# Three float16 products for the tiles' output projection, two weight groups prepared in each pooling tile, and the sample keys side by side

## The chip, the cores and the metric

The kernel runs on one core of a Trainium2 chip. The metric is the device time of one execution in microseconds (us). The engines are TensorE (PE: matmuls, with their weight loads in a row of their own, PEld), VectorE (DVE), ScalarE (ACT), GpSimd (POOL), and SyncE (SP), whose queue issues most of the transfers. The engines run apart and wait for one another by semaphores; each executes its own instructions in the order in which they are written.

## What is computed

One inference step of a decoder of two layers, for a prompt of 2048 tokens and for a sample group of 8 x 8 tokens, with shared weights (width 1024). Each layer has one combined input projection, a token mixer, a cross-attention over 256 memory tokens, gates, and one output projection that is added to the residual:

```python
z = rms_norm(x, norm_a[i]) @ w_in_a[i]                      # 1024 -> 2048
u, gp, qm, gm = jnp.split(z, [POOL_W, 2 * POOL_W, 2 * POOL_W + MEM_W], axis=-1)
yp = pool_mixer(u_ext, pos, pool_mix_w[i], pool_scale[i]) * jax.nn.silu(gp)
ym = memory_branch(qm, gm, mem_q_norm[i], mem_k[i], mem_v[i])
x = x + jnp.concatenate([yp, ym], axis=-1) @ w_out_a[i]     # 1024 -> 1024
...
q = rope_partial(rms_norm(q.reshape(B, T, N_Q_HEADS, HEAD_DIM), q_norm[j]), pos)
o = swa_banded(q, k, v, sinks[j])            # sample group: swa_window over 128 cached + 8 new keys
ys = o * jax.nn.silu(gq)
x = x + jnp.concatenate([ys, ym], axis=-1) @ w_out_b[j]
```

Layer A mixes by pooling windows of 2, 4, 8 and 16 tokens; layer B by a sliding window of 128 tokens with sinks. All inputs and outputs are float32.

## The kernel before

The program has five parts, one after the other: a prologue ("pre": memory keys and values, the splitting of layer A's input weights), loop A (8 pooling tiles of 256 prompt tokens), the sample block of layer A (SA), loop B (8 window tiles) and the sample block of layer B (SB). Values lie feature-major, 128 partitions x 8 chunks x 256 tokens.

**The input projections** are already taken as three float16 products: a float32 weight group (1024 x 256, 1 MB) and the normalised inputs are each split into a high and a low float16 part, and high x high, high x low and low x high are summed in PSUM (`split_features`, L623; the query part `qm` of a pooling tile is L794). The parts of layer B's weights are made during loop A, one group of 1 MB in each pooling tile: SP loads it into `stage_b` (L486), GpSimd multiplies it by the norm's gain (`gained`, L2055), ScalarE takes magnitudes (L1200), a TensorE matmul spreads the largest of all to every partition (`largest`, L633), VectorE makes a scale of it, ScalarE and VectorE write the high and the low part (L1137, L1511), and SP stores them to HBM (L489).

**The output projection** (`by_feature`, L649; its first half group L823 in a pooling tile and L1027 in a window tile) is in float32: 4 output groups `out0` to `out3` of 2 halves x 8 chunks, 64 matmuls 128x128x256 in a tile. `add_outputs` (DVE, L1596) adds each group to the residual.

**Order.** Nothing schedules at run time: each engine's stream is written by hand, and rings of PSUM banks are handed on by semaphores (Z for projections, T for transposes and totals, S for scores, V for values). A pooling tile on TensorE is `qm`, `u0` to `u2`, query transposes, `g0` with the memory scores in it, `g1`, `g2` and `gm` with transposes in them, memory values, `out0` to `out3`. During the output groups the next tile's input is squared (ACT, L1110), summed (GpSimd, `sums`, L2031 to L2035), its square sums go through TensorE (`square_sums`, "ss", L589), GpSimd takes the power (L2026), and a second matmul (`rstd_rows`, "rb", L600) spreads the result; VectorE and ScalarE then write the next tile's normalised high and low parts (L1472/L1476, L1132, L1482).

## Time and profile before

| | |
|---|---|
| time, median of 3 runs | 1806.86 us (1805.43 to 1807.42) |
| the profiled execution | 1804.33 us, span 1802.5 us, mean granted TensorE clock 0.968 of full |
| TensorE busy | 1687.7 us (94% of the span) |
| VectorE, ScalarE, GpSimd busy | 700.3, 504.8, 458.4 us (39, 28, 25%) |
| prologue, up to the first pooling tile | 119.7 us |
| loop A, each tile | 77.1 us |
| sample block A | 79.6 us |
| loop B, each tile | 109.1 us |
| sample block B | 111.2 us |

The span is the part of the time in which the profile shows the engines at work; the rest lies around it. A tile's period is read from the start of its first projection to the start of the next tile's. Busy shares are averages over stages with different limits, so each stage is read by itself.

### The profile page before, as it was taken

The numbers are of one execution on the slowest core, as the hardware profiler recorded it, in microseconds if no ns is written. First come the engines' busy times: TensorE is split into PE (matmuls) and PEld (weight loads), VectorE is DVE, ScalarE is ACT, GpSimd is POOL, SyncE is SP. The second block draws the span as 40 slices with busy tenths as digits, with TensorE's granted clock in tenths as the row PEclk, the third lists the DMA queues.
The fourth block names the chain that finished last, engine by engine and source line by source line (L and its number), as shares of the span: only waits on it lengthen the run. The fifth ranks groups of instructions, "written<-read, shape, count | busy, mean of one in ns | idle before, by whom it ended". The sixth has DMA issues, their size and how long they took to land.

```text
span 1802.5 us, 29285 instructions
## 1 busy us (share of the span) xinstructions
PE 1687.7 (94%) x11586; PEld 1286.4 (71%) x11586; DVE 700.3 (39%) x1621; ACT 504.8 (28%) x1236; POOL 458.4 (25%) x344
## 2 busy tenths in 40 slices
PE   5769999999999999869999999999999999999967
PEld 3648888888888888734767757677675776757753
DVE  3643241422424233213624436353452634536320
ACT  3343132231322223112504224142331514215110
POOL 0214134141422414212313123031321313223010
PEclk9789999999999999989999999999999999999976
DMA  9132201102020120565010010100001010010211
GB/s 367 55 120 86 94 25 72 57 38 95 13 83 25 71 94 1 186 266 229 1 47 1 2 48 2 47 1 27 23 1 47 1 48 1 1 47 1 101 50 47
DMA packets 23477, 113.60 MB, mean 63 GB/s; under 512 B 2551, under 2 KB 2999, under 8 KB 12550
## 3 DMA queue, kind: packets, MB, share of 16 engines
q1 hardware_dynamic: 22046, 102.87, 14.8%
q10 hardware_dynamic: 1296, 8.76, 1.2%
q8 instruction: 106, 1.74, 0.4%
q14 instruction: 29, 0.24, 0.0%
HBM read 80.24 MB, written 33.44 MB: 63 GB/s over the span
## 4 chain that ended last, share of the span: by engine, by line
PE 45%; issue 36%; POOL 13%; DVE 2%; DMA 2%; ACT 1%; POOLq 0%; SPq 0%; ACTq 0%; DVEq 0%
PE ps_z L623 17%; PE ps_z L649 12%; POOL tiny_sb L2026 4%; POOL ph_sb L2147 3%; PE ps_z L794 2%; PE ps_z L640 2%; POOL pm_sb L2050 2%; POOL pm_sb L2061 2%; PE ps_z L823 2%; POOL big_sb L2031 1%; PE ps_z L612 1%; PE ps_t L589 1%; PE ps_s L661 1%; PE ps_p L679 1%; PE ps_t L669 1%
## 5 line engine op out<-in xcount | busy, mean ns | idle before, releaser
L623 PE MATMUL ps_z<-xn_sb,w_in_sb 128*128 128x256 f16 (+1 forms) x4752 | 499.8, 264 | 0.8 <-DVE pm_sb L1527 0.8
L623 PEld LDWEIGHTS ps_z<-xn_sb,w_in_sb 128*128 128x128 f16 x4752 | 426.6, 98 | 62.1 <-issue 14.7
L649 PE MATMUL ps_z<-gate_sb,w_out_sb 128*128 128x256 f32 x1792 | 396.0, 380 | 0.0
L649 PEld LDWEIGHTS ps_z<-gate_sb,w_out_sb 128*128 128x128 f32 x1792 | 337.4, 190 | 44.2
L2026 POOL TENSOR_TENSOR tiny_sb<-tiny_sb 128x2 f32<-128x2 f32 (+4 forms) x56 | 94.1, 1681 | 777.7 <-DVE tiny_sb L1533 595.0
L612 PE MATMUL ps_z<-w_in_sb,xn_sb 128*128 128x512 f16 (+2 forms) x840 | 181.7, 376 | 0.0
L1118 ACT ACTIVATE scr_sb<-ps_z,tiny_sb 128x256 f32<-128x256 f32 (+2 forms) x94 | 42.5, 489 | 408.8 <-PE ps_z L612 314.2
L612 PEld LDWEIGHTS ps_z<-w_in_sb,xn_sb 128*128 128x128 f16 (+1 forms) x840 | 82.9, 99 | 94.2 <-issue 0.3
L1596 DVE TENSOR_TENSOR x_buf_sb<-x_buf_sb,ps_z 128x512 f32<-128x512 f32 x64 | 44.0, 687 | 250.4 <-PE ps_z L649 250.4
L1524 DVE TENSOR_REDUCE tiny_sb<-scr_sb 128x8 f32<-128x512 f32 (+3 forms) x64 | 38.0, 594 | 239.2 <-ACT scr_sb L1118 166.1
L1551 DVE TENSOR_REDUCE tiny_sb<-ps_s 128x4 f32<-128x1024 f32 x32 | 39.0, 1219 | 171.2 <-PE ps_s L661 171.2
L1132 ACT ACTIVATE xn_sb<-big_sb 128x2048 f16<-128x2048 f32 x18 | 34.4, 1910 | 226.7 <-DVE big_sb L1476 148.7
L1353 ACT ACTIVATE ph_sb<-ph_sb,tiny_sb 128x128 f32<-128x128 f32 x192 | 74.6, 390 | 68.0 <-DVE tiny_sb L1868 68.0
L612 PE MATMUL ps_z<-w_x_sb,xn_sb 128*128 128x512 f16 (+1 forms) x408 | 89.8, 379 | 0.1
L2147 POOL TENSOR_TENSOR ph_sb<-ph_sb,tiny_sb 128x512 f32<-128x512 f32 x48 | 49.9, 1041 | 152.9 <-DVE tiny_sb L1878 152.9
L2061 POOL TENSOR_TENSOR pm_sb<-pm_sb,tiny_sb 128x1024 f32<-128x1024 f32 x32 | 60.2, 1893 | 93.9 <-DVE tiny_sb L1559 93.9
L1566 DVE SCALAR_TENSOR_TENSOR gate_sb<-scr_sb,ps_z 128x512 f32<-128x512 f32 (+1 forms) x72 | 45.9, 638 | 85.8 <-ACT scr_sb L1149 85.3
L1160 ACT ACTIVATE pm_sb<-ps_s,tiny_sb 128x256 f32<-128x256 f32 x128 | 58.5, 474 | 56.8 <-DVE tiny_sb L1554 56.8
L612 PEld LDWEIGHTS ps_z<-w_x_sb,xn_sb 128*128 128x128 f16 (+1 forms) x408 | 39.9, 98 | 47.8 <-issue 1.3
L2031 POOL TENSOR_TENSOR big_sb<-big_sb 128x1024 f32<-128x1024 f32 x17 | 39.9, 2350 | 121.6 <-ACT big_sb L1110 121.6
L1149 ACT ACTIVATE scr_sb<-ps_z,tiny_sb 128x512 f32<-128x512 f32 (+1 forms) x72 | 46.9, 651 | 80.0 <-PE ps_z L623 78.7
L1154 ACT ACTIVATE big_sb<-ps_t 128x512 f32<-128x512 f32 (+1 forms) x68 | 39.6, 582 | 95.1 <-PE ps_t L669 69.9
(262 smaller groups left out, 2091.3 us busy)
## 6 DMA issues: line engine op xcount, KB each, us to landing
x_buf_sb<-x SPq DMA_DIRECT2D x18, 1024.0 KB, 4.9
x<-x_buf_sb SPq DMA_DIRECT2D x9, 1024.0 KB, 3.9
y<-x_buf_sb SPq DMA_DIRECT2D x9, 1024.0 KB, 4.0
w_x_sb<-w_in_b SPq DMA_DIRECT2D x8, 1024.0 KB, 6.7
w_in_sb<-parts ACTq DMA_DIRECT2D x8, 1024.0 KB, 11.0
w_out_sb<-w_mem SPq DMA_DIRECT2D x4, 1024.0 KB, 18.7
w_out_sb<-w_out_a SPq DMA_DIRECT2D x4, 1024.0 KB, 8.2
parts<-ph_sb SPq DMA_DIRECT2D x8, 512.0 KB, 3.1
```

The lines of the kernel that those rows point to most:

```text
L612: last = mm(out, xs[:, x, kc, tok:tok + n], w[:, gs[0]:gs[-1] + 1, ws, kc, :], start=(kc == 0 and ws + x == 0), stop=(kc == KC - 1 and ws ...
L623: last = mm(ps_z[:, b, half * NT:half * NT + n], w_split[:, g, ws, kc, half * P:(half + 1) * P], xs[:, x, kc, 0:n], start=(kc == 0 and ws ...
L649: last = mm(ps_z[:, b, half * NT:half * NT + n], w[:, g, kc, half * P:(half + 1) * P], src[:, kc, 0:n], start=(kc == 0), stop=(kc == KC - 1))
L1149: f(pair[0], pair[1], ACT.Tanh, scale=halfunit).then_inc(scr_in.sem, 1)
L1160: last = f(pm[:, blk, e, :], ps_s[:, b, e // 2, (e % 2) * NMEM:(e % 2 + 1) * NMEM], ACT.Exp, bias=m_neg[:, blk, e:e + 1], scale=SCALE, acc ...
L1353: f(sw[:, n % 2, e, :], sw[:, n % 2, e, :], ACT.Exp, bias=w_neg[:, n % 2, e:e + 1], scale=SCALE, accum_out=w_sum[:, n % 2, e:e + 1])
L1566: ve.scalar_tensor_tensor(gate[:, c:c + 2, 0:n], pair[0], 1.0, pair[1], ALU.add, ALU.mult)\
L1596: ve.tensor_tensor(x, x, ps_z[:, b].rearrange("p (c n) -> p c n", c=2)[:, :, 0:n], ALU.add)\
L2026: return tt(out, x, power[0:n, 0:w], ALU.pow)
L2031: own(tt(big[:, 0:4], big[:, 0:4], big[:, 4:8], ALU.add))
L2061: tt(pm[:, blk], pm[:, blk], r, ALU.mult).then_inc(pm_norm.sem, 1)
L2147: tt(sw[:, i], sw[:, i], r, ALU.mult).then_inc(pw_norm.sem, 1)
```

## The change

1. The tiles' output projection is taken as three float16 products (`split_outputs`): the output weights are split once (layer A's 4 groups at the end of the prologue, layer B's in loop A, stored with the others), and each tile's gated values are split by ScalarE (`gate_high`) and VectorE (`gate_low`) in four pairs of chunks. 64 float32 matmuls of a tile become 192 float16 ones.
2. Loop A prepares two weight groups in each tile (16 slots: 8 input groups, the shared K/V and 4 output groups of layer B) and does so at the tile's start: both groups are loaded behind the next tile's x, GpSimd multiplies by the gain, VectorE takes the largest of each row (`row_top_of`), ScalarE squares and accumulates (`row_squares`), and a TensorE matmul between `u1` and `u2` adds over partitions (`totals`).
3. Square sums in loop A come after the whole of `out0`; the spread ("rb") after `out1`. In loop B they come after `out0` and `out1`, and the spread after `out2`.
4. In the prologue the same row tops take the place of ScalarE's magnitudes, and GpSimd's gain passes are gone.
5. The sample blocks keep the float32 output projection and load its weights for it: in SA 4 MB and the pooling mix (0.75 MB) come ahead of the state projection's second weight group.
6. In SB old and new keys lie side by side (136 columns for each batch), so that scores take one matmul pair where there were two, and the new values one matmul for each key pair instead of one for each batch; the memory attention comes ahead of the window's values.

The sync engine's queue:

```diff
+            def prepare(t):
+
+                for s in range(2):
+                    sp.wait_ge(parts_out.sem, parts_out.after("A", t, -1))
+                    dma(stages[s], one_slot(io["w_b"], t * 2 + s).rearrange("a p k n -> (a p) k n"))\
+                        .then_inc(stage_in[s].sem, 16)
+                for s in range(2):
+                    out = one_slot(io["parts"], t * 2 + s).rearrange("a p s k n -> (a p) s k n")
+                    for half in range(2):
+                        sp.wait_ge(low_in.sem, low_in.after("A", t, 2 * s + half))
+                        dma(out[:, :, half * 4:half * 4 + 4, :], parts_b[s][half])\
+                            .then_inc((parts_out if s + half else first_out).sem, 16)
 
...
+            sp.wait_ge(parts_out.sem, parts_out.total)
+            sp.wait_ge(first_out.sem, first_out.total)
+            dma(w_x[:, 0:1536], io["mix"]).then_inc(mix_reload, 16)
+            dma(stages[1], io["w_u"][0]).then_inc(wu_in, 16)
...
+            Z.wait_full(sp, "A", TILES - 1, "out3")
+            for g in range(4):
+                dma(w_out[:, g], io["w_out_a"][g]).then_inc(wout_in[g], 16)
```

TensorE, the new functions, a pooling tile and the end of a window tile:

```diff
+            def totals(part, t, k, name, parts):
+
+                pe.wait_ge(top_sum.sem, top_sum.after(part, t, k))
                 T.wait_free(pe, part, t, name)
...
+                mm(ps_t[:, 0:parts.shape[1]], ones[:, :], parts, start=True, stop=True).then_inc(T.full[0], 1)
...
+            def split_outputs(part, t, name, g, chunks=range(KC), halves=(0, 1), first=True, last=True):
+
+                b = Z.wait_free(pe, part, t, name) if first else Z.bank(part, name)
+                for half in halves:
+                    for kc in chunks:
+                        for ws, x in PARTS:
+                            start = first and half == 0 and kc == chunks[0] and ws + x == 0
+                            done = mm(ps_z[:, b, half * NT:(half + 1) * NT],
+                                      w_out_split[:, g, ws, kc, half * P:(half + 1) * P], gated_parts[:, x, kc, :],
+                                      start=start, stop=last and half == 1 and kc == chunks[-1] and ws == 1,
+                                      skip_group_check=True)
+                if last:
+                    done.then_inc(Z.full[b], 1)
+
+            def wait_gated(part, t, k):
+                pe.wait_ge(gated_low.sem, gated_low.after(part, t, k))
```

```diff
-                    for i in range(3):
-                        split_features("A", t, f"u{i}", 1 + i)
+                    split_features("A", t, "u0", 1)
+                    split_features("A", t, "u1", 2)
+                    totals("A", t, 1, "top", w_top)
+                    split_features("A", t, "u2", 3)
...
-                    for g in range(4):
-                        pe.wait_ge(wout_in[g], 32)
-                    pe.wait_ge(pool_gated.sem, pool_gated.after("A", t))
-                    b = Z.wait_free(pe, "A", t, "out0")
-                    for kc in range(KC):
-                        if kc == POOLC:
-                            V.wait_read(pe, "A", t, "pvm")
-                        mm(ps_z[:, b, 0:NT], w_out[:, 0, kc, 0:P], gate[:, kc, :], start=(kc == 0), stop=(kc == KC - 1))
-                    largest("A", t, 0, "top0")
-                    by_feature("A", t, "out0", gate, w_out, 0, halves=(1,))
+                    pe.wait_ge(low_in.sem, low_in.after("pre", 0, 11))
+                    wait_gated("A", t, 0)
+                    split_outputs("A", t, "out0", 0, (0, 1), last=False)
+                    wait_gated("A", t, 1)
+                    split_outputs("A", t, "out0", 0, (2, 3), first=False, last=False)
+                    wait_gated("A", t, 2)
+                    split_outputs("A", t, "out0", 0, (4, 5), first=False, last=False)
+                    wait_gated("A", t, 3)
+                    split_outputs("A", t, "out0", 0, (6, 7), first=False)
```

```diff
                     window_transposes(t, 4)
-                    V.wait_read(pe, "B", t, "pvw2")
-                    first_output((0, 1, 6))
+                    wait_gated("B", t, 1)
+                    split_outputs("B", t, "out0", 0, (0, 1, 6, 7), last=False)
                     window_values(t, p, 4)
                     window_transposes(t, 5)
-                    V.wait_read(pe, "B", t, "pvw3")
-                    first_output((7, 2, 3))
+                    wait_gated("B", t, 2)
+                    split_outputs("B", t, "out0", 0, (2, 3), first=False, last=False)
+                    split_outputs("B", t, "out1", 1, (0, 1), last=False)
                     window_values(t, p, 5)
-                    V.wait_read(pe, "B", t, "pvw5")
-                    first_output((4, 5))
-                    by_feature("B", t, "out0", gate, w_out, 0, halves=(1,))
+                    split_outputs("B", t, "out1", 1, (6, 7, 2, 3), first=False, last=False)
+                    wait_gated("B", t, 3)
+                    split_outputs("B", t, "out0", 0, (4, 5), first=False)
+                    split_outputs("B", t, "out1", 1, (4, 5), first=False)
                     square_sums(V, "B", t, "ss", 0)
-                    project_out("B", t, (1,))
+                    project_out("B", t, (2,))
                     rstd_rows("B", t, "rb", 0)
```

ScalarE:

```diff
+            def gate_high(part, t, k, pair):
+                if part == "A" and pair < 3:
+                    act.wait_ge(gated.sem, gated.after(part, t, pair))
+                else:
+                    V.wait_read(act, part, t, ("pvw1", "pvw3", "pvw5", "pvm")[pair])
+                f(gated_parts[:, 0, PAIRS[pair], :], gate[:, PAIRS[pair], :], ACT.Copy).then_inc(gated_high.sem, 1)
```

```diff
+                    pooled_inputs(0)
+                    row_squares(row_tops[:, 0, :], w_top[:, 0:1], "A", t, 0, 0)
+                    row_squares(row_tops[:, 1, :], w_top[:, 1:2], "A", t, 1, 1)
+                    pooled_inputs(1)
+                    high_b(t, 0, 0)
+                    high_b(t, 0, 1)
+                    pooled_inputs(2)
                     from_t("A", t, "qT", qT_a[:, :, :], ps_t[:, :].rearrange("p (c n) -> p c n", c=2))
+                    high_b(t, 1, 0)
...
+                    gate_high("A", t, 0, 0)
+                    gate_high("A", t, 1, 1)
+                    gate_high("A", t, 2, 2)
                     tanh("A", t, "gm", halfunit_a[:, 7:8])
-                    magnitudes(t)
+                    gate_high("A", t, 3, 3)
```

VectorE:

```diff
+            def gate_low(part, t, k, pair):
+                dve.wait_ge(gated_high.sem, gated_high.after(part, t, k))
+                ve.tensor_tensor(gated_parts[:, 1, PAIRS[pair], :], gate[:, PAIRS[pair], :], gated_parts[:, 0, PAIRS[pair], :],
+                                 ALU.subtract).then_inc(gated_low.sem, 1)
...
+                    for s in range(2):
+                        dve.wait_ge(w_gained.sem, w_gained.after("A", t, s))
+                        row_top_of("A", t, s, row_tops[:, s, :], stages[s])
+                    power_from("A", t, 0, "top", w_power)
+                    scale_from("A", t, 0, w_power, w_scale, [(unit_b[:, bass.ds(t * 2, 2)], w_power, 1.0 / X_UNIT)])
+                    low_b(t, 0, 0)
+                    low_b(t, 0, 1)
                     for blk in range(NBLK):
                         mem_max("A", t, blk)
+                    low_b(t, 1, 0)
                     for blk in range(NBLK):
                         mem_inverse("A", t, blk)
-
-                    dve.wait_ge(parts_out.sem, parts_out.after("pre", 0, 1))
+                    low_b(t, 1, 1)
...
-                    window_differences(t)
-                    mix_gated("A", t)
+                    gate_low("A", t, 0, 0)
+                    mix_gated(t, 2)
+                    gate_low("A", t, 1, 1)
+                    gate_low("A", t, 2, 2)
                     silu("A", t, "gm", 4, 6)
                     mem_gated("A", t)
-                    weight_top("A", t, 0)
-                    weight_scale("A", t, 0, "top0", unit_b[:, bass.ds(t, 1)])
```

GpSimd:

```diff
+            def gained(t, s):
+
+                pool.wait_ge(stage_in[s].sem, stage_in[s].after("A", t))
+                gains = sm("slotgain")[:, bass.ds((t * 2 + s) * KC, KC)]
+                tt(stages[s], stages[s], gains.rearrange("p (k n) -> p k n", n=1).to_broadcast([P, KC, 256]), ALU.mult)\
                     .then_inc(w_gained.sem, 1)
+
...
+                    gained(t, 0)
                     heads("A", t, 0, q_rstds[0][:, 0:8], q_of(0)[:, 0:8, :], unit_a[:, 0:1].to_broadcast([P, 8]))
+                    gained(t, 1)
+                    weight_power("A", t, 0, w_power)
```

TensorE in SB, the window's values:

```diff
+                mm(ps_p[:, 0:384].rearrange("p (b n) -> p b n", b=DB), v[0:NS, 0, kp * P:(kp + 1) * P], pt_new[:, :, cols],
+                   start=True, stop=False, skip_group_check=True)
                 for n in range(DB):
-                    out = ps_p[:, n * 48:(n + 1) * 48]
-                    mm(out, v_old[:, n, kp * P:(kp + 1) * P], pt_old[:, n, cols], start=True, stop=False)
-                    last = mm(out, v_new[:, n, kp * P:(kp + 1) * P], pt_new[:, n, cols], start=False, stop=True)
+                    last = mm(ps_p[:, n * 48:(n + 1) * 48], v_old[:, n, kp * P:(kp + 1) * P], pt_old[:, n, cols],
+                              start=False, stop=(n == DB - 1), skip_group_check=True)
                 last.then_inc(V.full[0], 1)
```

How the order moves. TensorE from `qm` to the query transposes in a pooling tile, before (`ps_z` holds projections, `ps_t` transposes and totals):

```order
L794 MATMUL ps_z<-w_in_sb,xn_sb 128x256 x47
L623 MATMUL ps_z<-xn_sb,w_in_sb 128x256 [waits z_free1]
L623 MATMUL ps_z<-xn_sb,w_in_sb 128x256 x47
L124 REGISTER_ALU
L623 MATMUL ps_z<-xn_sb,w_in_sb 128x256 [waits z_free0]
L623 MATMUL ps_z<-xn_sb,w_in_sb 128x256 x47
L623 MATMUL ps_z<-xn_sb,w_in_sb 128x256 [waits z_free1]
L623 MATMUL ps_z<-xn_sb,w_in_sb 128x256 x47
L776 REGISTER_ALU
L124 ISA [waits heads_norm]
L780 MATMUL ps_t<-small_sb,pm_sb 128x128 [waits t_free]
L780 MATMUL ps_t<-small_sb,pm_sb 128x128 x3
```

and now:

```order
L654 MATMUL ps_z<-xn_sb,w_in_sb 128x256 x47
L128 REGISTER_ALU
L654 MATMUL ps_z<-xn_sb,w_in_sb 128x256 [waits z_free0]
L654 MATMUL ps_z<-xn_sb,w_in_sb 128x256 x47
L662 ISA
L128 ISA [waits top_sum]
L664 MATMUL ps_t<-tiny_sb,ones_sb 128x2 [waits t_free]
L654 MATMUL ps_z<-xn_sb,w_in_sb 128x256 [waits z_free1]
L654 MATMUL ps_z<-xn_sb,w_in_sb 128x256 x47
L832 REGISTER_ALU
L128 REGISTER_ALU [waits heads_norm]
L836 MATMUL ps_t<-small_sb,pm_sb 128x128 [waits t_free]
```

Between the second and the third pooled projection stands a matmul of 128x2 that waits for the row sums of both weight groups (`top_sum`).

GpSimd from a pooling tile's first instruction, before (`pm_sb` holds queries and memory weights, `ph_sb` the pooling windows):

```order
L2026 TENSOR_TENSOR tiny_sb<-tiny_sb 128x8 [waits heads_var]
L163 ISA
L2047 TENSOR_TENSOR tiny_sb<-tiny_sb 128x8 [waits pool_steps]
L163 REGISTER_ALU
L2050 TENSOR_TENSOR pm_sb<-pm_sb,tiny_sb 128x512 [waits pool_steps]
L134 ISA
L2105 TENSOR_TENSOR ph_sb<-ph_sb 128x6x270 [waits z_free0,z_free1]
L163 REGISTER_ALU
L2107 TENSOR_TENSOR ph_sb<-ph_sb 128x5x268 [waits pool_steps]
L2059 ISA
L2061 TENSOR_TENSOR pm_sb<-pm_sb,tiny_sb 128x1024 [waits m_inv_in]
```

and now:

```order
L2234 ISA [waits stage_in0]
L2234 TENSOR_TENSOR w_x_sb<-w_x_sb,small_sb 128x2048
L2220 REGISTER_ALU
L2203 TENSOR_TENSOR tiny_sb<-tiny_sb 128x8 [waits heads_var]
L167 ISA
L2224 TENSOR_TENSOR tiny_sb<-tiny_sb 128x8 [waits pool_steps]
L167 REGISTER_ALU
L2227 TENSOR_TENSOR pm_sb<-pm_sb,tiny_sb 128x512 [waits pool_steps]
L2234 ISA [waits stage_in1]
L2234 TENSOR_TENSOR w_x_sb<-w_x_sb,small_sb 128x2048
L138 ISA
L2203 TENSOR_TENSOR tiny_sb<-tiny_sb 128x2 [waits t_free]
```

Two gain passes over 128x2048 and a power stand ahead of the windows, the first of them ahead of the query heads; the pass that stood behind the windows is gone.

TensorE at the last windows of a window tile, before (`ps_p` holds window values):

```order
L942 MATMUL ps_t<-small_sb,ph_sb 128x128 [waits t_free,pw_norm]
L942 MATMUL ps_t<-small_sb,ph_sb 128x128 x3
L1027 MATMUL ps_z<-gate_sb,w_out_sb 128x256 [waits p_free]
L1027 MATMUL ps_z<-gate_sb,w_out_sb 128x256 x2
L134 REGISTER_ALU
L124 REGISTER_ALU [waits t_free]
L954 MATMUL ps_p<-ph_sb 64x128 [waits p_free]
L954 MATMUL ps_p<-ph_sb 64x128 x7
L939 REGISTER_ALU
L942 MATMUL ps_t<-small_sb,ph_sb 128x128 [waits t_free,pw_norm]
L942 MATMUL ps_t<-small_sb,ph_sb 128x128 x3
L1027 MATMUL ps_z<-gate_sb,w_out_sb 128x256 [waits p_free]
```

and now:

```order
L685 REGISTER_ALU
L128 REGISTER_ALU [waits gated_low]
L677 MATMUL ps_z<-pm_sb,w_out_sb 128x256 [waits z_free0]
L677 MATMUL ps_z<-pm_sb,w_out_sb 128x256 x23
L138 REGISTER_ALU
L128 REGISTER_ALU [waits t_free]
L1013 MATMUL ps_p<-ph_sb 64x128 [waits p_free]
L1013 MATMUL ps_p<-ph_sb 64x128 x7
L998 REGISTER_ALU
L1001 MATMUL ps_t<-small_sb,ph_sb 128x128 [waits t_free,pw_norm]
L1001 MATMUL ps_t<-small_sb,ph_sb 128x128 x3
L685 REGISTER_ALU
```

The first output matmuls now wait for the low parts of the gated values (`gated_low`), 24 of them in a row stand ahead of the fifth window's values.

## Rows read from the trace of the kernel before

**Rows 1.** Windows: start:end, length, busy by engine, clock, DMA share, GB/s.

```profile
0.00:119.92 119.92, 77.56 (x251) 51.31 (x252) 64.55 (x116) 48.80 (x45) 14.35 (x14) 0.86 0.39 160
430.16:507.29 77.13, 77.13 (x576) 67.48 (x575) 26.03 (x55) 19.68 (x35) 24.45 (x16) 1.00 0.14 56
739.12:818.73 79.61, 58.94 (x560) 35.71 (x559) 14.28 (x40) 13.04 (x29) 14.77 (x26) 0.87 0.69 262
1036.76:1145.90 109.14, 106.15 (x711) 75.86 (x711) 49.11 (x121) 33.67 (x103) 28.02 (x21) 1.00 0.06 20
1691.30:1802.50 111.20, 84.73 (x523) 53.73 (x522) 20.67 (x58) 14.45 (x53) 9.73 (x8) 0.74 0.22 80
```

**Rows 2.** TensorE's timeline in pooling tile 4: start, busy, operation, count.

```profile
430.00 5.40 PE L794 MATMUL ps_z<-w_in_sb,xn_sb 128*128 128x256 f16 x48
435.24 15.88 PE L623 MATMUL ps_z<-xn_sb,w_in_sb 128*128 128x256 f16 x144
...
493.31 13.98 PE L649 MATMUL ps_z<-gate_sb,w_out_sb 128*128 128x256 f32 x64
```

**Rows 3.** Sync engine's queue, same tile, and the page's issues (median us to landing).

```profile
435.60 0.33 SPq L486 DMA_DIRECT2D w_x_sb<-w_in_b  x1
...
w_x_sb<-w_in_b SPq DMA_DIRECT2D x8, 1024.0 KB, 6.7
```

**Rows 4.** GpSimd's timeline, same tile.

```profile
437.60 1.64 POOL L2026 TENSOR_TENSOR tiny_sb<-tiny_sb 128x8 f32<-128x8 f32 x1 [27.65 <-DVE tiny_sb L1533]
439.59 1.04 POOL L2050 TENSOR_TENSOR pm_sb<-pm_sb,tiny_sb 128x512 f32<-128x512 f32 x1
...
467.35 3.60 POOL L2055 TENSOR_TENSOR w_x_sb<-w_x_sb,small_sb 128x2048 f32<-128x2048 f32 x1
480.79 2.35 POOL L2031 TENSOR_TENSOR big_sb<-big_sb 128x1024 f32<-128x1024 f32 x1 [9.84 <-ACT big_sb L1110]
...
484.56 0.73 POOL L2035 TENSOR_TENSOR big_sb<-big_sb 128x256 f32<-128x256 f32 x1
```

**Rows 5.** VectorE's and ScalarE's timelines, same tile.

```profile
487.51 1.28 DVE L1511 SCALAR_TENSOR_TENSOR ph_sb<-w_x_sb,tiny_sb,ph_sb 128x1024 f16<-128x1024 f32 x1
...
501.02 2.28 DVE L1482 TENSOR_TENSOR xn_sb<-big_sb,xn_sb 128x2048 f16<-128x2048 f32 x1
...
478.81 1.90 ACT L1110 ACTIVATE big_sb<-x_buf_sb 128x2048 f32<-128x2048 f32 x1
```

**Rows 6.** GpSimd's and VectorE's timelines in a window tile.

```profile
1094.71 1.89 POOL L2061 TENSOR_TENSOR pm_sb<-pm_sb,tiny_sb 128x1024 f32<-128x1024 f32 x1 [4.17 <-DVE tiny_sb L1559]
...
1095.76 0.86 DVE L1876 TENSOR_TENSOR tiny_sb<-tiny_sb 128x4 f32<-128x4 f32 x1 [0.70 <-ACT tiny_sb L1355]
...
1103.65 0.16 DVE L1876 TENSOR_TENSOR tiny_sb<-tiny_sb 128x4 f32<-128x4 f32 x1 [1.42 <-ACT tiny_sb L1355]
```

**Rows 7.** Windows in the prologue, and TensorE's first pooling projection.

```profile
75.10:77.40 2.30, 0.00 (x0) 0.01 (x1) 2.20 (x4) 2.30 (x2) 0.00 (x0) 1.00 0.00 0
78.50:82.00 3.50, 3.24 (x9) 2.13 (x7) 3.50 (x4) 0.14 (x1) 0.00 (x0) 0.51 0.00 0
...
119.72 7.00 PE L794 MATMUL ps_z<-w_in_sb,xn_sb 128*128 128x256 f16 x48
```

**Rows 8.** TensorE's and VectorE's timelines where a window tile ends.

```profile
1112.87 1.46 PE L1027 MATMUL ps_z<-gate_sb,w_out_sb 128*128 128x256 f32 x6
...
1113.07 1.29 DVE L1886 TENSOR_TENSOR ph_sb<-ps_t,small_sb 128x512 f32<-128x512 f32 x2
```

**Rows 9.** TensorE's waits in the first sample block.

```profile
PE ps_z L724 <- DMA w_x_sb<-w_u: 7.4, 1, 7.4
```

**Rows 10.** Groups by line, TensorE, in the second sample block.

```profile
L1091 PE MATMUL ps_p<-w_in_sb,w_x_sb 128*128 128x48 f32 x32 | 10.6, 431 | 2.6 <-DVE gate_sb L2011 1.5 <-DVE w_in_sb L2000 1.1
L1092 PE MATMUL ps_p<-w_in_sb 8*128 8x48 f32 x32 | 10.5, 426 | 0.0
L1066 PE MATMUL ps_s<-ph_sb,w_in_sb 128*96 128x8 f32 x32 | 5.3, 308 | 1.9 <-ACT w_in_sb L1194 1.9
```

668 lines of the change are left out of this document (390 added, 278 removed).

## The prediction

> **What bounds the kernel now.** I read the page's busy shares first, then windows for each stage, since the share is an average over five different parts. [rows 1] give one pooling tile, one window tile and the three blocks outside the loops. In a pooling tile TensorE is busy 77.13 of 77.13 us; VectorE, ScalarE and GpSimd have 26.0, 19.7 and 24.5 us of work. There nothing but TensorE counts, and its time falls only if its instructions get shorter and nothing makes it wait. In a window tile it is busy 106.15 of 109.14. In the first sample block it is busy 58.9 of 79.6 with the DMA engines at 0.69, in the second 84.7 of 111.2 at a clock of 0.74: waits set those. So the view to ask next is the timeline of one tile, in order to see which chain could reach TensorE late.
>
> **The output projection.** [rows 2] have both kinds of matmul on 128x128x256. The float32 row has two records for each matmul, so its 64 records are 32 matmuls in 13.98 us, 0.437 us each. 144 float16 ones take 15.88 us, 0.110 each, at the same clock of 1.00. Old: 64 x 0.437 = 28.0 us in a tile. New: 192 x 0.110 = 21.1. That is **-6.9 us** in a pooling tile. In a window tile, where the first half group was cut into pieces of three and two matmuls at 0.487 ([rows 8]: 6 records in 1.46), 28.4 becomes 21.1: -7.3. Sixteen tiles would give 114 us if no wait came with it.
>
> **The wait for the two weight groups.** The totals matmul stands between `u1` and `u2`, and TensorE takes instructions in order: all of `u2` and the rest of the tile queue behind it. With E the start of `qm`, `u0` starts at E+5.24 and a group of 48 takes 5.23 [rows 2], so TensorE is there at E+15.7. The operand comes by this chain: the x load must wait for the x store of the tile that just ended, so the queue reaches the weight load at E+5.60 [rows 3], and its median landing time is 6.7 us. Two loads now share the queue; I put 0.7 on the first: landed at E+13.0. Then GpSimd in its written order: gain 3.60, query heads 3.03 (437.60 to 440.63), gain 3.60 [rows 4], E+23.2. Row tops of the second group on VectorE: no such row; the nearest of 2048 elements takes 2.28 [rows 5], E+25.5. Squares and accumulation of 128x8 on ScalarE, about 0.4, and two handoffs: E+26.3. TensorE stands **10.6 us**. Bounds: 8.8 (the first load alone, a cheaper reduction) and 12.8 (row tops held up behind GpSimd). None of it can move into the tile before, since the loads follow the store that follows the last `out3`.
>
> **After a wait the clock is low.** In [rows 7] TensorE did nothing for 2.30 us, and the stretch just after ran at 0.51, which is 1.2 GHz instead of 2.4. The first pooling projection, after 11.65 us without work, took 7.00 where the same 48 matmuls take 5.40 in tile 4: 1.6 us lost. I charge **+1.6** for the 10.6 us wait (bounds 0.5 to 3). The Trainium skill says the same of idle time in "TensorE: Matmul & The Clock Gate" (Part 1: The HAM clock gate); by it a cold array runs at 1.2 GHz; the trace agrees, with 0.51 after 2.30 us idle, and the 7.00 us row is already the price.
>
> **Further on in the pooling tile.** (a) The squares of the next x now stand on ScalarE behind `gate_high` of the last pair, which waits for the memory branch: they end at about 481.9 on the old axis, and the sums take 4.5 more (480.79 to 485.29, [rows 4]), to 486.4. TensorE, which comes to `out0` at 478.1 and now some 0.4 later (b), has finished all of it, 48 x 0.110, at 483.75: a wait of **+2.65** where there was none, and about +0.9 for the clock (half of the 1.7 that a full low stretch would cost). (b) `g2` waits for `silu g0`, which VectorE does behind the fourth low part: **+0.4**. (c) That low part reads two SBUF tiles. In [rows 6] a 128x4 VectorE instruction with two SBUF inputs takes 0.86 instead of 0.16: it ends at 1096.62, and the GpSimd instruction that it lay beside ends at 1096.60. The low part (1.28, [rows 5]) falls beside the memory normalisation on GpSimd, 1.89 each: **+1.2** (0 if it meets a gap). The Trainium skill has this as a lock, in "SBUF — State Buffer" (Who interferes with whom): a VectorE instruction with two SBUF inputs and a GpSimd one that reads SBUF exclude each other until the first ends; the trace agrees to 0.02 us, and without that rule the tile would be 1.2 shorter. (d) The low part of the next x is ready about 2 us before `out3` ends: no wait.
> Sum for a pooling tile: -6.9 + 10.6 + 1.6 + 2.65 + 0.9 + 0.4 + 1.2 = **+10.45**, 77.1 to 87.6. Seven tiles: **+73**.
>
> **Prologue and first tile.** Four more weight groups are split after the first 8 (ScalarE 1.90, VectorE 2.28 each, [rows 5]), and the queue's loop starts only when the last is done. I put that at 133 (119.7 and four times 2.3, behind some 4 us of totals and heads); then 7 us to the landing and the chain above, 14 us, so `u2` of tile 0 starts at about 154.8 where it now starts at 137.0 (119.72 and 6.83 for `qm` [rows 7], two groups of 5.23): **+17.8**, with 4 either way. The rest of that tile is -6.9 and the terms (a) to (c), -0.1 with a low-clock wait: -0.1.
>
> **First sample block.** 4 MB of output weights and 0.75 MB of mix stand in the queue ahead of the state projection's second group. TensorE already waits 7.4 us there for such a group [rows 9]; at some 400 GB/s the new bytes are 12 us, of which the wait at the value slots later on (the block has 20 us without TensorE work) absorbs part. I take **+4.5** (1 to 10).
>
> **Window tiles.** Besides -7.3, four small waits at the window outputs (1.1 together, of the 3.0 us idle in [rows 1]) go. New: the first 24 matmuls want the low part of pair 3, which VectorE does behind the weights of window 4: these end at 1114.36 ([rows 8], 1113.07 + 1.29), plus 0.7 for the subtraction, 1115.1, and TensorE is there at 1112.87: **+2.2**. Queued behind on TensorE are the values of windows 4 and 5; nobody else waits for them so early. The spread after `out2` leaves only `out3` (5.3 us) to cover VectorE 2.28, ScalarE 1.90 and VectorE 2.28 [rows 5] plus handoffs, 6.8: **+1.55**. Clock after the 2.2: 0.9 (0 to 1.7). Sum -3.75, eight tiles: **-30** (-24 to -39).
>
> **Second sample block.** 64 value matmuls [rows 10] of 0.43 become 16 + 2 wider pairs: from 21.1 us to about 12. The two score passes become one over 136 columns: some 5 us of the 5.3 [rows 10]. Gates fill waits at the transposes, some 4 us; the merged softmax and the memory waits give a few back: **-11** (-5 to -16).
>
> **Sum.** +73 + 17.8 - 0.1 + 4.5 - 30 - 11 = +54.2 on the profiled 1804.3: 1858.5. The median of the runs shown lies 2.5 above the profiled execution, so **1861 us**. Differences under 0.2% (3.6 us) can't be told from none.
>
> **Rivals.**
> *The chain is short (faster).* If the operand reached TensorE by E+20 (loads that land sooner, GpSimd passes that overlap), the wait would be 4 us and, at a wait that short, the clock loss about half: a tile gains 0.4 + what (a) leaves, so it is about +3; with B and SB at their better ends and the first tile at +12 that is 21 + 12 + 2 - 36 - 14 = -15: about 1792. It decides at a wait of about 3.5 us in a tile with the other terms as forecast, at 5.5 with all of them at those better ends. Against it: [rows 3] and [rows 4] alone, without any of VectorE's work, put the chain at E+23.2. **0.13.**
> *No clock loss.* The array keeps 2.4 GHz after the waits: 8 x 2.5 in A and 8 x 0.9 in B less, 27 us: about 1833. Against it stand both kinds of stretch in [rows 7]. **0.12.**
> *The waits cost more.* Row tops or the low parts meet GpSimd's passes more often, and the wait is at 12.8: seven tiles at +13, and B loses 3 more at its `gate_low` subtractions, which also read two SBUF tiles: about 1890. **0.15.**
> *The products gain nothing*: 192 float16 matmuls behind `gate_low` waits are as slow as 64 float32 ones; then 114 us more, near 1970. Against it the 0.110 of [rows 2], from the very same shape: **0.02.**
>
> **How the numbers follow.** The forecast has 0.58; by itself its bounds give 1840 to 1880. The range that leaves out no more than 2 in 10 takes in the case without clock loss and the costly one, and reaches toward the short chain: 1808 to 1892. Faster by over 0.2%: the first rival, 0.13. Same: 0.04, taken from the low end of the second. Slower: 0.83.
>
> **What would show it.** In the profile after: output matmuls at about 0.110; in each pooling tile a wait of 9 to 13 us on TensorE ahead of the totals matmul, put down to ScalarE's row sums or to what feeds them, with a clock near 0.5 after it; a wait of 2 to 3 at the square sums; tiles of 86 to 89; window tiles of 104 to 107. I am wrong if the totals wait is under 5 us, if a window tile's new waits exceed 7, or if the second sample block does not get shorter.

## The result, and the profile after

The changed kernel takes **1885.86 us** in the median of four runs (1878.95 to 1888.27) where the kernel before takes 1806.14: a ratio of 1.044, with an interval of 1.042 to 1.046. It is slower, as forecast; 1861 was named, within 1808 to 1892. The profiled execution took 1888.27 us.

The page of the kernel after opens like this:

```profile
span 1886.4 us, 31792 instructions
...
PE 1610.1 (85%) x12555; PEld 1203.0 (64%) x12555; DVE 814.6 (43%) x1733; ACT 544.3 (29%) x1344; POOL 500.5 (27%) x365
```

Its windows (columns as in [rows 1]) are, in order: prologue, pooling tiles 0, 1 and 4, the first sample block, one window tile, the second sample block.

```profile
0.00:121.73 121.73, 73.50 (x254) 48.47 (x255) 67.55 (x114) 42.99 (x52) 12.78 (x17) 0.88 0.45 179
121.73:213.86 92.13, 76.39 (x639) 64.80 (x640) 44.75 (x86) 26.46 (x45) 30.70 (x19) 0.89 0.15 60
213.86:304.08 90.22, 74.04 (x640) 63.43 (x638) 37.05 (x62) 22.67 (x43) 29.70 (x18) 0.92 0.18 71
484.42:574.23 89.81, 74.94 (x638) 63.99 (x639) 35.54 (x60) 22.56 (x43) 29.70 (x18) 0.90 0.18 71
841.27:929.18 87.91, 59.14 (x560) 36.10 (x559) 14.42 (x40) 13.06 (x29) 14.82 (x26) 0.84 0.76 293
1035.49:1142.09 106.60, 100.78 (x773) 71.00 (x773) 51.98 (x125) 36.16 (x108) 28.04 (x21) 0.98 0.06 21
1786.42:1886.40 99.98, 71.22 (x463) 40.62 (x463) 19.17 (x57) 15.56 (x57) 10.04 (x9) 0.79 0.36 131
```

A pooling tile was 77.1 us of TensorE without a gap at a clock of 1.00. It is now about 90, of which TensorE works 74 to 75, at 0.90 to 0.92. So the work shrank by less than the forecast 6.9 us, since some of it runs at the low clock, and 15 us of waiting came in. The window tile shown is 2.5 shorter, the second sample block 11.2, the first sample block 8.3 longer.

TensorE's timeline of pooling tile 1 shows where they stand (in brackets: the idle time ahead of the row and what ended it):

```profile
213.86 5.40 PE L850 MATMUL ps_z<-w_in_sb,xn_sb 128*128 128x256 f16 x48
219.10 10.64 PE L654 MATMUL ps_z<-xn_sb,w_in_sb 128*128 128x256 f16 x96
240.52 0.58 PE L664 MATMUL ps_t<-tiny_sb,ones_sb 128*128 128x2 f32 x2 [10.78 <-ACT tiny_sb L1273]
240.97 6.67 PE L654 MATMUL ps_z<-xn_sb,w_in_sb 128*128 128x256 f16 x48
...
262.04 2.79 PE L654 MATMUL ps_z<-xn_sb,w_in_sb 128*128 128x256 f16 x24 [1.02 <-DVE gate_sb L1667]
...
283.97 0.61 PE L620 MATMUL ps_t<-ones_sb,big_sb 128*128 128x1 f32 x4 [2.74 <-POOL big_sb L2212]
284.44 7.07 PE L677 MATMUL ps_z<-pm_sb,w_out_sb 128*128 128x256 f16 x48
...
304.08 0.61 PE L850 MATMUL ps_z<-w_in_sb,xn_sb 128*128 128x256 f16 x4 [1.65 <-issue]
```

The chain behind the 10.78 us, in the timelines of the sync engine's queue, GpSimd, VectorE and ScalarE for the same tile:

```profile
214.98 0.38 SPq L525 DMA_DIRECT2D x<-x_buf_sb  x1
219.04 0.35 SPq L522 DMA_DIRECT2D x_buf_sb<-x  x1
219.68 2.14 SPq L508 DMA_DIRECT2D w_x_sb<-w_b  x2
...
227.49 3.60 POOL L2234 TENSOR_TENSOR w_x_sb<-w_x_sb,small_sb 128x2048 f32<-128x2048 f32 x1 [28.68 <-DMA w_x_sb<-w_b]
...
234.06 3.60 POOL L2234 TENSOR_TENSOR w_x_sb<-w_x_sb,small_sb 128x2048 f32<-128x2048 f32 x1
...
237.69 2.29 DVE L1591 TENSOR_REDUCE tiny_sb<-w_x_sb 128x8 f32<-128x2048 f32 x1 [4.28 <-POOL w_x_sb L2234]
...
240.21 0.19 ACT L1273 ACTIVATION_READ_ACCUMULATOR tiny_sb<-tiny_sb 128x1 f32 x1
```

It is read backwards: totals at 240.52, row sums until 240.40, row tops until 239.98, the second gain pass until 237.66, the first from 227.49, when its load landed, and that load was issued at 219.68, since the x load ahead of it had to wait until the x store (214.98) was done. The two passes, the query heads between them and the row tops are in sequence; nothing in them is slow.

TensorE's waits over pooling tiles 1 to 7 and, behind the dots, over the window tiles (in total, times, longest):

```profile
PE ps_t L664 <- ACT tiny_sb L1273: 72.2, 7, 11.2
PE ps_t L620 <- POOL big_sb L2212: 19.2, 7, 2.7
PE ps_z L654 <- DVE gate_sb L1667: 7.1, 7, 1.0
PE ps_z L850 <- issue: 5.4, 3, 2.1
...
PE ps_z L677 <- DVE pm_sb L1616: 16.9, 8, 2.2
PE ps_z L643 <- DVE xn_sb L1588: 13.3, 8, 2.3
...
PE ps_z L643 <- issue: 5.8, 3, 2.0
```

The first three and the first two of the second part were forecast. The two rows "issue", 5.4 and 5.8 us, were not: TensorE waits for nothing that the profile shows, three times in each loop, just behind the loop's branch back, ahead of the first matmul in loop A and of the fifth in loop B (a loop body holds two tiles; the kernel before has 0.3 us of it at this line of loop A in all).

### The profile page after: what moved, and what is told of

It reads as the page before. It is cut to its first block, busy times and chain, and to the rows that moved or that the text cites. A ratio compares the mean times of both kernels' runs of the same rounds, so it can differ in the third digit from the quotient of the medians.

```text
span 1886.4 us, 31792 instructions
## 1 busy us (share of the span) xinstructions
PE 1610.1 (85%) x12555; PEld 1203.0 (64%) x12555; DVE 814.6 (43%) x1733; ACT 544.3 (29%) x1344; POOL 500.5 (27%) x365
## 4 chain that ended last, share of the span: by engine, by line
PE 41%; issue 21%; DVE 15%; POOL 11%; DMA 7%; ACT 4%; SPq 0%; POOLq 0%; DVEq 0%; ACTq 0%
PE ps_z L677 15%; PE ps_z L643 14%; DMA w_x_sb<-w_b 3%; PE ps_z L654 3%; DVE ph_sb L2055 2%; PE ps_z L691 2%; DVE ph_sb L2028 2%; ACT ph_sb L1443 2%; DVE tiny_sb L2031 2%; DMA x<-x_buf_sb 2%; POOL w_x_sb L2234 2%; POOL pm_sb L2245 1%; POOL tiny_sb L2203 1%; POOL ph_sb L2296 1%; POOL big_sb L2208 1%
## 5 line engine op out<-in xcount | busy, mean ns | idle before, releaser
L654 PE MATMUL ps_z<-xn_sb,w_in_sb 128*128 128x256 f16 (+1 forms) x4752 | 519.0, 270 | 8.6 <-DVE gate_sb L1667 8.1
L654 PEld LDWEIGHTS ps_z<-xn_sb,w_in_sb 128*128 128x128 f16 x4752 | 437.0, 101 | 79.3 <-issue 14.7
L677 PE MATMUL ps_z<-pm_sb,w_out_sb 128*128 128x256 f16 x3072 | 366.0, 282 | 16.9 <-DVE pm_sb L1616 16.9
L677 PEld LDWEIGHTS ps_z<-pm_sb,w_out_sb 128*128 128x128 f16 x3072 | 308.9, 102 | 66.8 <-issue 23.3
L2203 POOL TENSOR_TENSOR tiny_sb<-tiny_sb 128x8 f32<-128x8 f32 (+4 forms) x70 | 106.4, 1519 | 581.2 <-DVE tiny_sb L1634 267.8
L2234 POOL TENSOR_TENSOR w_x_sb<-w_x_sb,small_sb 128x2048 f32<-128x2048 f32 x16 | 57.6, 3603 | 231.3 <-DMA w_x_sb<-w_b 231.3
L1705 DVE SCALAR_TENSOR_TENSOR x_buf_sb<-ps_z,tiny_sb,x_buf_sb 128x512 f32<-128x512 f32 x64 | 47.9, 748 | 116.0 <-PE ps_z L677 116.0
L664 PE MATMUL ps_t<-tiny_sb,ones_sb 128*128 128x2 f32 (+3 forms) x28 | 6.9, 314 | 93.6 <-ACT tiny_sb L1273 84.8
L1591 DVE TENSOR_REDUCE tiny_sb<-w_x_sb 128x8 f32<-128x2048 f32 x17 | 38.8, 2285 | 108.0 <-POOL w_x_sb L2234 108.0
L664 PEld LDWEIGHTS ps_t<-tiny_sb,ones_sb 128*128 128x128 f32 x28 | 6.2, 267 | 98.3 <-issue 87.1
## 6 DMA issues: line engine op xcount, KB each, us to landing
w_in_sb<-parts ACTq DMA_DIRECT2D x8, 1024.0 KB, 11.1
```

The lines of the kernel that those rows point to most:

```text
L654: last = mm(ps_z[:, b, half * NT:half * NT + n], w_split[:, g, ws, kc, half * P:(half + 1) * P], xs[:, x, kc, 0:n], start=(kc == 0 and ws ...
L677: done = mm(ps_z[:, b, half * NT:(half + 1) * NT], w_out_split[:, g, ws, kc, half * P:(half + 1) * P], gated_parts[:, x, kc, :], start=sta ...
L1705: ve.scalar_tensor_tensor(x, ps_z[:, b].rearrange("p (c n) -> p c n", c=2)[:, :, 0:n], out_unit[part][:, g:g + 1], x, ALU.mult, ALU.add).t ...
L2203: return tt(out, x, power[0:n, 0:w], ALU.pow)
L2234: tt(stages[s], stages[s], gains.rearrange("p (k n) -> p k n", n=1).to_broadcast([P, KC, 256]), ALU.mult)\
```

## The experiments

Two theories were held against each other. **T1**: the loss comes from the waits of the forecast, each from the place where an edit put a step; move the step and the time comes back. **T2**: the float16 products bring the loss themselves (low clock, stalls at the branch, more matmuls behind each handoff), and it stays when the waits go. Ratios are to the kernel before on the same chip (1802.2 to 1803.6 us).

**1. Weight loads ahead of the store.** Both loads are issued behind the parts of the tile before, and the two gain passes run without the query heads between them; in the last tile two spare slots are loaded that nobody uses.

```diff
                     prepare(t)
+                    load_stages(t + 1)
...
                     gained(t, 0)
-                    heads("A", t, 0, q_rstds[0][:, 0:8], q_of(0)[:, 0:8, :], unit_a[:, 0:1].to_broadcast([P, 8]))
                     gained(t, 1)
+                    heads("A", t, 0, q_rstds[0][:, 0:8], q_of(0)[:, 0:8, :], unit_a[:, 0:1].to_broadcast([P, 8]))
```

> The changed kernel with the two weight loads of a pooling tile issued in the tile before (behind the stores of its weight parts, ahead of the x store), and GpSimd's two gain passes one behind the other ahead of the query heads. Theory (the wait at the totals is made by loads that follow the x store, and GpSimd's passes behind them): the 10.8 us wait ahead of the 128x2 totals matmul goes in tiles 1 to 7, and with it most of the low clock behind it (1.4 to 2.0); a pooling tile falls from 89.6 to about 77.3, tile 0 by about 3 (heads no longer stand in its chain), the whole to about 1797 us. Rival (the wait is VectorE's or ScalarE's place in the order, not the load): TensorE still waits over 5 us there and the kernel stays above 1840.

Measured: **1810.10 us**, ratio 1.003 (1.001 to 1.005), 76 us less than the changed kernel. Tiles 1 to 7 take 77.9 to 80.2 us. Its waits over the pooling tiles and the first sample block no longer have the totals matmul, and have one new row:

```profile
PE ps_t L629 <- POOL big_sb L2221: 19.2, 7, 2.7
PE ps_s L902 <- DMA x_buf_sb<-mem_ks: 12.1, 1, 12.1
PE ps_z L663 <- DVE gate_sb L1676: 9.0, 7, 1.3
PE ps_p L640 <- DVE diag_sb L1567: 7.3, 5, 3.0
```

The new wait is a collision that the early passes bring. VectorE's timeline in the changed kernel, then VectorE's and GpSimd's here, all in tile 1:

```profile
285.59 0.48 DVE L1558 TENSOR_SCALAR diag_sb<-small_sb,tiny_sb 128x128 f32<-128x128 f32 x2 [0.81 <-POOL tiny_sb L2203]
...
271.01 7.18 DVE L1567 TENSOR_SCALAR diag_sb<-small_sb,tiny_sb 128x128 f32<-128x128 f32 x2 [0.81 <-POOL tiny_sb L2212]
...
270.95 7.16 POOL L2243 TENSOR_TENSOR w_x_sb<-w_x_sb,small_sb 128x2048 f32<-128x2048 f32 x2
```

Two instructions that take 0.48 us together in the changed kernel take 7.18 here and end with the two gain passes beside them (278.19 and 278.11). The Trainium skill says in "SBUF — State Buffer" (Who interferes with whom) that a `tensor_scalar` can enter a mode with two ports, and that it and GpSimd then exclude each other for a whole instruction; this trace agrees, to 0.08 us. In experiment 6, where the passes wait until the diagonals are made, the row is gone. So T1 holds for the largest term. Of the 12 us by which tiles 1 to 7 miss the expectation, 7.3 are this wait and 1.9 a longer one ahead of `g2` (9.0 instead of 7.1); the rest was not taken apart.

**2. Squares ahead of the last high part.** ScalarE squares the next x before it makes `gate_high 3`.

```diff
-                    gate_high("A", t, 3, 3)
                     V.wait_full(act, "A", t, "pvm")
                     squares_x("A", t, 0, 1 - p, it * 16 + 32)
+                    gate_high("A", t, 3, 3)
```

> The changed kernel with ScalarE's squares of the next x ahead of the last gate_high in a pooling tile. Theory (the 2.74 us wait at the square sums comes from squares that stand behind gate_high of pair 3): the squares start about 1.8 us earlier, the wait falls to about 0.9 and the low clock behind it (1.67 in most tiles) goes in most tiles; 8 tiles by about 2.8 each, to about 1863 us. Rival (the last piece of out0 waits for its low part instead): the wait moves to the output matmuls and the time stays within 5 us of 1886.

Measured: 1868.43, 1.036 (1.034 to 1.038). TensorE's timeline in tile 1:

```profile
279.81 1.48 PE L677 MATMUL ps_z<-pm_sb,w_out_sb 128*128 128x256 f16 x12 [0.95 <-DVE pm_sb L1616]
281.73 0.61 PE L620 MATMUL ps_t<-ones_sb,big_sb 128*128 128x1 f32 x4 [0.43 <-POOL big_sb L2212]
282.20 5.40 PE L677 MATMUL ps_z<-pm_sb,w_out_sb 128*128 128x256 f16 x48
```

Of the 2.74 us wait 0.43 is left, 0.95 moved to the last quarter of `out0`, whose low part now comes later, and the next 48 matmuls are at 5.40 again instead of 7.07: 3.0 us in this tile. Tiles 1 to 7 got shorter by 2.2 us each, since the totals wait, which no line of this edit touches, was 0.7 a tile longer in this execution (77.3 us instead of 72.2). The clock's part, 1.67, is more than the forecast's 0.9.

**3. Padding at the branch.** Six float32 matmuls of 256 columns, into a result that nobody reads, at the end of each second pooling tile: 10 us more work in all, in order to see whether the "issue" time hides behind queued work.

```diff
+                    if p == 1:
+                        for _ in range(6):
+                            mm(ps_t[:, 0:NT], ones[:, :], gate[:, 0, :], start=True, stop=True)
```

> The changed kernel with six further float32 matmuls 128x128x256, whose result nobody reads, at the end of loop A's body on TensorE (every second tile, ahead of the branch back): 6 x 0.437 = 2.6 us of work in four places. Theory (the 1.65 to 2.13 us in which TensorE stands behind the branch, waiting for nothing shown, is time in which its sequencer gets to the new instructions, and short float16 matmuls leave too little queued work to cover it): the gap ahead of the query projection in tiles 2, 4 and 6 goes or falls under 0.5, and the total grows by only some 3 to 5 us. Rival (the gap is a fixed cost at that place or a wait for another engine): the gap stays at 1.6 to 2.1 and the total grows by 10.5.

Measured: 1871.83, 1.037 (1.035 to 1.040): more work, 14 us less time than 1885.86. The theory nearly holds: the "issue" time ahead of tiles 2, 4 and 6, 5.4 us before, is

```profile
PE ps_z L850 <- issue: 1.8, 3, 0.9
```

with 2.6 us of float32 matmuls ahead of the branch. The kernel before also has float32 matmuls there, and no stall. (The padding moves the code behind it too, but experiment 4 moves the code alone and keeps 6.0 us.) So this stall does come with the short products. Two more things happened that were not asked for. The totals wait in tiles 2, 4 and 6 is 6.4 to 6.7 us, where the changed kernel has 11.2, 11.1 and 6.3; but the same kernel run once more has 6.4, 6.6 and 11.2 without padding, so this is not shown to be the padding's work. And loop B, in which no line differs, lost its three stalls at the fifth matmul and went from 857.2 to 846.5 us. So these depend on something that changes when code ahead of them grows.

**4. Code shifted.** Six matmuls of one column, ahead of loop A, do nothing but move the instructions behind them. 30 of them move the same code further.

```diff
+            for _ in range(6):
+                mm(ps_p[0:64, 0:1], ones[:, 0:64], ones[:, 0:1], start=True, stop=True)
```

> The changed kernel with six tiny matmuls (12 instructions, 0.1 us each at most) on TensorE ahead of loop A, in the prologue, that write a PSUM bank nobody uses then: the loop bodies are the same, only moved in the program. Theory (the stalls behind the branches depend on where in the program's memory the instructions lie, which is how padding loop A alone took 11 us off loop B): the stalls of 1.7 to 2.0 behind the fourth matmul of the window tiles 2, 4 and 6 go, and the total falls by 8 to 12 us; in loop A they change place or size. Rival (loop B was faster in the padded run for another reason, its store or its waits): the stalls stay as in the changed kernel and the time stays within 3 us of it.

> The changed kernel with 30 tiny matmuls (60 instructions) ahead of loop A where the earlier run had 6. Theory (where a stall behind a branch falls hangs on the position of the instructions in program memory): the stalls of loop A or B sit at another matmul than the first and the fifth, or one of the two loops loses or gains one; the total differs from the run with 6 (1870) by several us. Rival (anything ahead of the loops takes the stalls of loop B away, or the difference was one of chip and run): the same picture as with 6.

> The changed kernel once more, as it is, beside the next two on one chip: 1880 to 1888 us by its earlier runs, with the same stalls behind the branches (1.65 to 2.13 in loop A, 1.7 to 2.0 in loop B).

Measured: **1869.95** (1.036, 1.034 to 1.038) with six, **1872.33** (1.038, 1.036 to 1.041) with 30, and the changed kernel once more 1883.78 (1.045, 1.042 to 1.047). The rows for "issue" in loop A, of the kernel with six and of the one with 30:

```profile
PE ps_z L853 <- issue: 6.0, 3, 2.2
```

```profile
PE ps_z L853 <- issue: 10.6, 6, 2.3
```

In loop B neither has any such row, and B takes 846.3 and 846.1 us, where the changed kernel took 857.2 and, run once more, 854.3: 8 to 11 us. What went is the stall at the fifth matmul. The one ahead of the first matmul stays in both loops; in B it lies inside the wait for the normalised inputs, which is 1.7 to 2.2 us behind a branch and 1.5 elsewhere. With 30, loop A has a second stall behind each branch, at the 25th matmul. So the second stall follows where the code lies, and the first does not.

The Trainium skill says in "Runtime: NRT & Kernel Launch" (Instruction fetch mechanics) that a taken branch to code that isn't at hand waits for a DMA fetch of it. The trace agrees as far as it goes: a packet of an instruction queue starts shortly before TensorE runs out of work. This is the queue's row (packets, MB, share) from 301.0 to 302.4 us in the changed kernel, whose TensorE works until 302.44 and then stands until 304.08:

```profile
q8 instruction: 1, 0.02, 4.2%
```

The kernel before has such a packet at the same branch (272.5 to 273.5 us) and no stall, for its TensorE works without a gap until the next tile begins at 275.73:

```profile
q8 instruction: 1, 0.02, 7.2%
```

The trace does not name the engine whose instructions come so. But the fetch stands at both branches, and with experiment 3 this says that the first stall comes where less work is left to cover it. No run here shows how much code is at hand, or what position makes a second stall. Loop A's tiles 1 to 7 take 622.1 us with six matmuls instead of 627.4, but kernels with an unchanged loop A took 624.2 (run once more) and 632.1 (the second kernel of experiment 5), so no gain there is shown.

**5. The end of a window tile.** The order of output pieces is changed so that pairs 0 and 3 come first and each waits only for its own low part, the square sums stand ahead of the last pair, and the spread stands in the middle of `out2`; VectorE takes the variance of x ahead of the first output sum.

```diff
-                    wait_gated("B", t, 1)
-                    split_outputs("B", t, "out0", 0, (0, 1, 6, 7), last=False)
+                    wait_gated("B", t, 0)
+                    split_outputs("B", t, "out0", 0, (0, 1), last=False)
+                    wait_gated("B", t, 1)
+                    split_outputs("B", t, "out0", 0, (6, 7), first=False, last=False)
...
+                    square_sums(V, "B", t, "ss", 0)
                     wait_gated("B", t, 3)
...
-                    project_out("B", t, (2,))
+                    split_outputs("B", t, "out2", 2, halves=(0,), last=False)
                     rstd_rows("B", t, "rb", 0)
+                    split_outputs("B", t, "out2", 2, halves=(1,), first=False)
```

> The changed kernel with three moves at the end of a window tile: the first 12 output matmuls wait only for the low part of pair 0 and the next 12 for that of pair 3; the square sums stand ahead of the last output pieces of out0 and out1; the spread of the result stands after the first half of out2. Theory (a window tile gains only 2.3 instead of 7.3 because of the 2.06 us wait for the low parts, the low clock after it, 1.7, and the 1.5 to 2.3 us wait for the next normalised inputs): the first wait falls to about 0.8, the clock stays up, the last wait goes; about 4.5 in a tile, 36 in eight, to about 1850 us. Rival (VectorE or ScalarE is late elsewhere in the same stretch, so the waits move): less than 10 us in all.

Measured: 1863.79, 1.0325 (1.031 to 1.034), where 1850 was expected. The first and the last window tile, which have no stall, take 101.6 us instead of about 106; the others take 103.3 to 103.6 or 106.1 to 108.9, as a part of a stall or most of it falls into them. The stalls behind a branch grew, from 5.8 to 17.0 us in the "issue" rows. The timelines of TensorE and the sync engine's queue:

```profile
1137.33 1.03 PE L643 MATMUL ps_z<-w_x_sb,xn_sb 128*128 128x512 f16 x4 [1.87 <-issue]
1142.85 12.34 PE L643 MATMUL ps_z<-w_x_sb,xn_sb 128*128 128x512 f16 x44 [4.48 <-issue]
...
1136.28 0.34 SPq L575 DMA_DIRECT2D y<-x_buf_sb  x1
```

The 1 MB y store goes out just as TensorE stalls. In a further kernel the store is held back until the next tile's first group is done:

```diff
+                    Z.wait_full(sp, "B", t + 1, "kv0")
                     dma(tile_of(yd, t), x_buf[:, 1 - p])
```

> The kernel with the new window end (1863.8 us) with the y store of a window tile held back until the next tile's first projection is complete, loop A untouched. Theory (instructions by DMA behind the store): the 6.3 us (1.9 and 4.5) that TensorE stands at the start of window tiles 2 and 6, and 4.5 at tile 4, fall to about 2; total 10 to 14 us less, about 1851. Rival (fixed cost, or a wait for another engine that the profile doesn't show): the stalls stay and the total stays within 3 us.

Measured: 1862.15, 1.031 (1.029 to 1.033). The "issue" rows of loop B, without and with the store held back:

```profile
PE ps_z L643 <- issue: 17.0, 6, 4.5
```

```profile
PE ps_z L644 <- issue: 11.0, 6, 2.3
```

So the store lengthens the stalls by 6 us over three branches; loop B gets 5.1 us shorter. The other 11 us are there without it: the 1.7 to 2.3 ahead of the first matmul, which the wait for the normalised inputs no longer hides, and the second stall. The whole got only 1.6 us shorter, not 10 to 14, and that lies within the spread of the runs.

**6. All together.** Edits 1, 2 and 5; GpSimd's gain passes wait until the diagonals are made; the output weights of loop A are loaded behind the first value slots of the sample block instead of ahead of them.

```diff
+                    pool.wait_ge(diag_x.sem, diag_x.after("A", t, -1))
                     gained(t, 0)
...
             for n in range(4):
                 load_slot(sp, "SA", n, 0, 1)
-            Z.wait_full(sp, "A", TILES - 1, "out3")
-            for g in range(4):
-                dma(w_out[:, g], io["w_out_a"][g]).then_inc(wout_in[g], 16)
...
             dma(stages[1], io["w_u"][2]).then_inc(wu_in, 16)
+            Z.wait_full(sp, "A", TILES - 1, "out3")
+            for g in range(4):
+                dma(w_out[:, g], io["w_out_a"][g]).then_inc(wout_in[g], 16)
             for n in range(12, 16):
```

> The early loads, the squares first and the new window end together, with two more edits: GpSimd's first gain pass waits until VectorE has written the diagonal tiles of the tile before (with the early loads alone TensorE stood 1.3 to 3.0 us for these, which I put down to the gain pass that VectorE's instruction lay beside), and the first sample block's output weights are loaded behind the third group of the state projection. If the waits were separate and of the sizes seen in the single runs: 1810 - 12 (diagonals) - 15 (squares) - 20 (window end) - 6 (sample block) = about 1757 us, below the kernel before. If they only pass one wait on to another: above 1790.

Measured: **1746.69**, 0.968 (0.966 to 0.970), 10 us under the sum of the single gains. Pooling tiles of 73.4 us, and 75.2 with a branch's stall at the end; the first sample block 80.2 instead of 87.9. Two variants followed: both stores held back, and the y store held back with the six matmuls of experiment 4.

> The combined kernel with the 1 MB store of a finished tile (x in loop A, y in loop B) held back until the next tile's first projection is complete. Theory (behind the branch of a loop TensorE waits for instructions that come by DMA, and these stand behind the store on the same DMA engines): the stalls ahead of and just behind the first projection of tiles 2, 4 and 6 (1.7 to 2.1 in loop A, 6.3 in loop B with the new window end) fall to 2 or less; about 10 to 15 us less than the combined kernel. Rival (the stalls are a fixed cost of the branch): no difference, or slower by what the later x loads cost.

> The combined kernel with the y store alone held back in loop B (the x store of loop A at its old place, since holding it back cost 7 us in the first sample block) and the six tiny matmuls ahead of loop A. Theory (position and store both stand behind the stalls): the window tiles behind a branch fall from 108.2 to about 104, loop A as in the combined kernel; about 12 us below its 1746.7, some 1735. Rival: the moved code puts the stalls elsewhere, 1742 to 1747.

Measured: 1744.43, 0.966 (0.9645 to 0.968), for the first, no clear gain over 1746.69: window tiles with a stall got 1.1 to 3.1 us shorter, but the last x store, held back, stands ahead of the sample block's loads in the queue: its first slot loads go out 8.7 us after the block's start instead of 5.6, and the block takes 87.6 instead of 80.2. The second took **1729.85**, 0.959 (0.957 to 0.961), the fastest kernel here. In its loop B the "issue" time falls from 18.0 us in six stalls to 6.6 in three: the first stalls are left. Its windows of pooling tile 2 and the first window tile:

```profile
280.55:353.95 73.40, 70.64 (x638) 61.73 (x639) 37.37 (x60) 22.66 (x43) 30.33 (x18) 1.00 0.23 86
811.16:912.74 101.58, 98.94 (x773) 70.17 (x773) 53.75 (x141) 35.85 (x107) 27.99 (x21) 1.00 0.22 84
```

The clock is back at 1.00, TensorE's work in pooling tile 2 is 70.6 us, 6.5 under the old 77.1, and 2.8 us of waits are left. T2 falls as the main cause: with the waits gone the products pay. What it has right is the first stall behind each branch.

## Why the prediction was right, point by point

**The wait for the two groups** was right in place, cause and size: E+26.66 for the totals in tile 1 where E+26.3 was worked out, and 72.2 us in seven tiles, 10.3 each, where 10.6 was forecast. Experiment 1 shows the cause: loads that don't follow the store, with the query heads' 3 us taken out from between the passes, remove it. The rival of a short chain is out.

**The clock** was right in kind, and so the rival without loss is out. After the long wait the 48 matmuls of `u2` took 6.67 to 7.73 us in tiles 1 to 7 where 5.40 is the price at full clock: 1.3 to 2.3 lost, 1.9 on average, forecast 1.6. After the wait at the square sums the loss is all or nothing: 1.67 in tiles 1 to 7 (7.07 instead of 5.40), and nothing in tile 0 behind a wait of the same length:

```profile
197.23 0.61 PE L620 MATMUL ps_t<-ones_sb,big_sb 128*128 128x1 f32 x4 [2.76 <-POOL big_sb L2212]
197.70 5.40 PE L677 MATMUL ps_z<-pm_sb,w_out_sb 128*128 128x256 f16 x48
```

The 0.9 that was charged, half of a figure that the rows before the change do not show, was too little here. In the window tiles, behind waits of 2.1 to 2.2, five tiles lost 1.67 and three nothing, 1.05 a tile where 0.9 was forecast; tiles 1 and 2:

```profile
1113.83 4.46 PE L677 MATMUL ps_z<-pm_sb,w_out_sb 128*128 128x256 f16 x24 [2.06 <-DVE pm_sb L1616]
...
1224.05 2.79 PE L677 MATMUL ps_z<-pm_sb,w_out_sb 128*128 128x256 f16 x24 [2.17 <-DVE pm_sb L1616]
```

What decides between the two, no run shows. Nor does the low stretch of [rows 7] stand just behind its wait, as the prediction reads it; 1.1 us of work at full clock lie between:

```profile
77.40:78.50 1.10, 1.07 (x5) 0.83 (x6) 1.10 (x1) 0.15 (x1) 0.00 (x0) 1.00 0.00 0
```

**The smaller terms of a pooling tile.** The wait at the square sums was 2.74, forecast 2.65. `g2` waited 1.02, where 0.4 and 1.2 were forecast: the low part did meet the memory normalisation, but took 2.09 instead of 1.28, 0.8 more. The sum was 87.6; tiles 1 to 7 take 627.4 us, 89.6 each. They lose 87 against the old 540.6, forecast 73. The missing 2 us a tile are the clock, the stalls (5.4 in seven tiles, 0.8 each) and the products, less 0.8 by which the three waits together were shorter than forecast. TensorE works 523.4 us in these tiles; the first kernel of experiment 6, at a clock of 1.00, works 495.1, and the kernel before 540.3. So the low clock took 4.0 a tile where 2.5 was forecast, and the products saved 6.5 instead of 6.9.

**Prologue and first tile** cost 15.4 us (213.86 against 198.44), forecast 17.7 (the working's own 133, 7 and 14 give 154.0 for `u2`, not 154.8). **The first sample block** cost 8.3, within its bounds of 1 to 10, but at another place than named: `w_u` still waits 6.9 [rows 9], and the wait for the key slots grew from 4.5 to 12.1, before and after:

```profile
PE ps_s L837 <- DMA x_buf_sb<-mem_ks: 4.5, 1, 4.5
...
PE ps_s L893 <- DMA x_buf_sb<-mem_ks: 12.1, 1, 12.1
```

The new bytes weren't absorbed by the slots; they are what the slots wait for: in experiment 6, with the weights behind them, this wait is 4.3 and the block takes 80.2 (84.1 in the fastest kernel, which waits 5.6 for the value slots). The prediction's 400 GB/s stands in no row; the 262 GB/s at a DMA share of 0.69 in [rows 1] make 380.

**Window tiles** are the term that was mis-sized: -15.4 us where -30, with bounds of -24 to -39, was forecast. The two waits were nearly right, 2.1 (2.2) and 1.7 (1.55), and so was the clock after the first. The stalls were not in the sum at all: 5.8 us of standing, and some 5 of low clock behind them (with the stall the first 48 matmuls of a tile take 14.0 to 14.3 us, in the others 10.5). Code shifted by six matmuls takes them away and gives 10.9 us back (8.1 against the changed kernel run once more), -26.3 in all, which is inside the bounds. The other 4 us are about 1 of clock after the first wait and about 3 of products that, by the fastest kernel's window tiles, saved 6.9 a tile instead of 7.3.

**The second sample block** gave 11.2, forecast 11, but its parts were rougher than that. The value matmuls saved 10.5 us (9 forecast; the 64 records of [rows 10] are 32 matmuls, with two records each), the scores 7.0 (5 forecast), and other work and waits gave some 6 back. That the sum agrees is partly luck.

In sum +2.0 and +13.4 ahead of tile 1, +87, +8.3, -15.4 and -11.2 make +84 between the profiled executions; forecast was +54. The clock (11 us more than forecast in A, 1 in B) and the stalls (5, and 11 with the low clock behind them) carry 28 of the 30 us between; the rest nearly cancels. So the direction, the main wait and its cause were right, but 1885.86 lies above the forecast's own 1840 to 1880, and the stated range holds it by the margin that was given to the costly rival. That rival came nearest in time, but not by its mechanism: its totals wait of 12.8 us and its hold in loop B did not come, and its terms add up to 1882 or 1903, not 1890, as its 3 us are taken for all of loop B or for each tile.

Open: what position of the code makes a second stall, and when a wait of 2 to 3 us costs clock.

## What to carry to other kernels

A cheaper instruction on the engine that sets the time is worth its saving only if whatever feeds that engine was early by more than the saving: list, for each operand of the next tile, how early it lands, before making the matmuls faster. When a tile needs one more load, put its issue ahead of the store that ends the tile before. And after moving a pass to GpSimd's free stretch, look at what VectorE does there.

## What was not expected of the hardware

Behind a loop's branch TensorE stood 1.6 to 2.1 us ahead of the first matmul of loop A where the loop ends in short float16 matmuls, 0.4 to 0.9 with 2.6 us of float32 matmuls put at its end, and at most 0.3 in the kernel before, which ends in float32 ones. A second stall, a few matmuls on, came and went with the position of the code: six tiny matmuls far ahead of loop B took it away (8 to 11 us), and 30 gave loop A one. It was up to 4.5 us long with a 1 MB store on the DMA engines beside it. And a wait of 2.1 to 2.8 us cost 1.7 us in clock behind it in 12 of 16 tiles and nothing in the other four, where one of 6 to 11 us always cost 1.3 to 2.3 (tiles 1 to 7).
